# Mask and maximum of attention scores in one VectorE instruction: a two-layer decoder step on one core

## The chip, the core and the metric

The kernel runs on one core of a Trainium2 chip. The metric is the time of the program on the device in microseconds (us). A profile is one execution taken by the hardware profiler; its times count from the start of its span. The engines are named PE (TensorE, matrix products), PEld (TensorE's weight loads), DVE (VectorE), ACT (ScalarE), POOL (GpSimd) and SP (SyncE, which issues most transfers). L2110 is line 2110 of the kernel before.

## The reference

Two decoder layers run over a prompt of 512 tokens and 8 samples of 8 new tokens each. In each layer three mixers read one projection of the normalised input: two gated linear recurrences and a dilated sliding-window attention of 8 heads of 64 channels. A channel mixer follows, dense in layer 0 and with experts in layer 1. The change touches the attention, cut here to what matters; each of three (window, dilation) patterns is one part, and the parts are combined by their softmax denominators:

```
s = einsum(q, k) * HEAD_DIM ** -0.5
s = where(valid, s, -inf)
m = max(s, axis=-1)
p = exp(s - m[..., None])
den = sum(p, axis=-1)
num = einsum(p, v)
```

The samples do the same against a cache of 1024 older keys and values and their own new ones.

## The kernel before

The three dilation patterns are folded into one softmax. The mask holds, for each query and key, the logarithm of the number of patterns in which the key counts, and -1e30 where there is none. These masks are constants in SBUF: `lnc` for the prompt, `smask` for a sample's 1024 cached keys, `smask_new` for the 64 new keys.

Attention is a hand-written schedule. Every engine has its own program, and semaphores tie them together. In each layer all engines run a loop over c = 0 to 9.

- The prompt's work is 16 steps n = 0 to 15: head pair n // 4 and query tile i = n % 4, with 128 (i + 1) keys for each of the two heads. TensorE computes the scores (`prompt_scores`, L1518), VectorE masks and reduces (`prompt_masked`, L2091 and L2093), ACT takes the exponential and its sum (`prompt_exp`, L1056), VectorE divides (`prompt_normed`, L2099 and L2101), TensorE transposes (`prompt_turn`, L1530), ACT copies out of PSUM (`prompt_turned`, L1066), TensorE multiplies with the values (`prompt_values`, L1542). Pass c starts steps 2c and 2c + 1.
- The sample's work is 8 steps b = c: scores against the cached keys (`sample_scores`, L1564), mask and maximum (`sample_masked`, L2108 to L2113), exponential (`sample_exp`, L1078), transposes (`sample_turn`, L1571 and L1574), copies (L1086 and L1087), product with the values (`sample_values`, L1584 and L1589).

Before, a prompt step's scores of both heads are scaled and masked by one `scalar_tensor_tensor` from PSUM into SBUF (tile Pp[i]), which then releases the PSUM scores through the semaphore `sc_free`; TensorE's next `prompt_scores` waits for it. A `tensor_reduce` over both heads follows, waits on `sc_free` too, writes the negated maxima and raises `mx_ready`, for which ACT waits. A sample step does the same over 1024 cached keys, with 64 masked new-key scores copied in behind them, so that its reduction runs over 1088 elements. The new-key scores of all samples are masked once per layer at c = 0 (L2137). TensorE fills gaps there with products whose results nothing reads (`idle_products`, L1290).

The cached keys and values come in pieces of 1 MB, four per sample (two of keys, two of values), through nine buffers; SP issues a piece (L608) when the last reader of its buffer has finished. VectorE also splits finished rows of the mixers into two parts (L2155) after ACT has made the first part (L1126). After the loop the output projection starts.

Of the kernel before, what the change touches and what calls it, by code (L numbers as in the profile page):

```python
# [23 lines left out]
ALU = mybir.AluOpType  # L24
ACT = mybir.ActivationFunctionType
AX = mybir.AxisListType

P = 128
# [121 lines left out]
def log_mult(dist, valid):  # L150
    n = np.where(valid, multiplicity(dist), 0)
    return np.where(n > 0, np.log(np.maximum(n, 1)), -1e30).astype(np.float32)


def shape_constants():
    c = {}
    p = np.arange(P)[:, None]

    u = np.arange(SEQ)[None, :]
    c["lnc"] = log_mult(SEQ - P + p - u, SEQ - P + p - u >= 0)  # L160
    row = p % 32
    t = row % DEC
    live = row < 2 * DEC
    d = PAST + t - np.arange(PAST)[None, :]
    c["smask"] = np.where(live, log_mult(d, d >= 0), 0).astype(np.float32)
    key = np.arange(NS)[None, :]
    new = []
    for b in range(NB):
        d = t - key % DEC
        new.append(np.where(live, log_mult(d, (d >= 0) & (key // DEC == b)), 0).astype(np.float32))  # L170
    c["smask_new"] = np.concatenate(new, 1)
    pos = np.concatenate([np.arange(SEQ), np.tile(PAST + np.arange(DEC), NB)]).astype(np.float32)
    rot_dim = DH // 4
    inv = (np.float32(500000.0) ** (-np.arange(0, rot_dim, 2, dtype=np.float32) / np.float32(rot_dim))).astype(np.float32)
    ang = pos[:, None] * inv[None, :]
    cos, sin = np.ones((P, T), np.float32), np.zeros((P, T), np.float32)
    rot = np.zeros((P, P), np.float32)
    for h in range(2):
        for i in range(rot_dim // 2):
            a, b = h * DH + i, h * DH + rot_dim // 2 + i  # L180
            cos[a] = cos[b] = np.cos(ang[:, i])
            sin[a] = sin[b] = np.sin(ang[:, i])
            rot[b, a] = -1.0
            rot[a, b] = 1.0
    c["cos"], c["sin"], c["rot"] = cos, sin, rot
    q = np.arange(P)[None, :]
    c["mask16"] = ((p // BLK == q // BLK) & (q >= p)).astype(np.float32)
    q = np.arange(NS)[None, :]
    c["mask8"] = ((p // DEC == q // DEC) & (q >= p)).astype(np.float32)
    c["ident"] = np.eye(P, dtype=np.float32)  # L190
    c["ones"] = np.ones((P, P), np.float32)
    c["bones"] = (p // DH == np.arange(P)[None] // DH).astype(np.float32)
    reset = np.ones(T, np.float32)
    reset[0:SEQ:P] = 0
    reset[SEQ::DEC] = 0
    c["reset"] = np.broadcast_to(reset[None], (P, T))
    c["maskb"] = (p // DEC == np.arange(NB)[None]).astype(np.float32)
    c["riota"] = np.broadcast_to(8.0 - np.arange(8)[None], (P, 8))
    c["before"] = (p < np.arange(P)[None]).astype(np.float32)
    c["slots"] = np.broadcast_to(np.arange(MAX_ITEMS)[None], (P, MAX_ITEMS))  # L200
    c["tokens"] = p + P * np.arange(TT + 1)[None]
    for nh in (4, 2):
        c[f"heads{nh}"] = (p // (P // nh) == np.arange(nh)[None]).astype(np.float32)
    q = np.arange(P + BLK - 1)[None, :] - (BLK - 1)
    c["to_row"] = (q == p // 32 * 32).astype(np.float32)
    c["of_row8"] = (p % 32 == np.arange(NS)[None] % DEC).astype(np.float32)
    c["of_row16"] = (p % 32 == np.arange(P)[None] % BLK).astype(np.float32)
    return np.ascontiguousarray(np.concatenate([c[n].astype(np.float32) for n, _ in CONSTS], 1))


def build(nc, d):

    ctx = ExitStack()
    with ctx:
# [3 lines left out]
        def sem(name):  # L218
            return ctx.enter_context(nc.semaphore(name))
# [126 lines left out]

        new_scores = V[:, 0, 0:NB * NS]
        Os = [V[:, 1 + b // 4, b % 4 * P:b % 4 * P + P] for b in range(NB)]
        s_negmax, s_den, s_rden = (SM[:, 2 * k:2 * k + 2] for k in range(3))
        Qs = LIN[:, 6144:7168].rearrange("p (b h q) -> p b h q", b=NB, h=4)  # L350

# [44 lines left out]
        def split(ap):  # L396
# [27 lines left out]
            "upd_done", "s_ready", "vbd_ready", "vbd_used", "supd_done", "sn_ready"))  # L424
        o_done, osq_ready, oss_done, orinv_ready, mixl_ready = (sem(n) for n in (
            "o_done", "osq_ready", "oss_done", "orinv_ready", "mixl_ready"))
        sc_done, sc_free, mx_ready, p_ready, pn_ready, pt_ps, pt_ready, pv_done, mixc_ready = (sem(n) for n in (
            "sc_done", "sc_free", "mx_ready", "p_ready", "pn_ready", "pt_ps", "pt_ready", "pv_done", "mixc_ready"))
        qs_ready, spv_half, os_ready, os_turned = (sem(n) for n in ("qs_ready", "spv_half", "sample_out_ready", "sample_out_turned"))
        ssc_done, ssc_free, smx_ready, sp_ready, spt_ps, spt_ready, spv_done, smix_ready = (sem(n) for n in (  # L430
            "ssc_done", "ssc_free", "smx_ready", "sp_ready", "spt_ps", "spt_ready", "spv_done", "smix_ready"))
        sig_ready = sem("sig_ready")
        mixhi_ready, mixlo_ready, ohi_ready, o_split = (sem(n) for n in (
            "mixed_hi_ready", "mixed_lo_ready", "out_weights_hi_ready", "out_weights_split"))
# [438 lines left out]
        def _(act):  # L873
# [31 lines left out]
            for L in range(DEPTH):  # L905
# [145 lines left out]
                def prompt_exp(n):  # L1051
                    if 0 <= n < N_STEP:
                        i = n % TT
                        act.wait_ge(mx_ready, n0 + n + 1)
                        for h in range(2):
                            op = nc.scalar.activation(Pp[i][:, h, :], Pp[i][:, h, :], ACT.Exp, bias=negmax[:, 2 * i + h:2 * i + h + 1],  # L1056
                                                      accum_out=den[:, 2 * i + h:2 * i + h + 1])
                        op.then_inc(p_ready, 1)

# [15 lines left out]
                def sample_exp(b):  # L1075
                    n = NB * L + b
                    act.wait_ge(smx_ready, n + 1)
                    nc.scalar.activation(Ps, Ps, ACT.Exp, bias=s_negmax[:, b % 2:b % 2 + 1],  # L1078
                                         accum_out=s_den[:, b % 2:b % 2 + 1]).then_inc(sp_ready, 1)

                def sample_turned(b):
# [182 lines left out]
        def _(pe):  # L1264
# [34 lines left out]
            for L in range(DEPTH):  # L1299
# [208 lines left out]
                def prompt_scores(n):  # L1508
                    if 0 <= n < N_STEP:
                        hp, i = n // TT, n % TT  # L1510
                        w = P * (i + 1)
                        if n >= 1:
                            pe.wait_ge(sc_free, n0 + n)
                        for c in range(0, w, 256):
                            e = min(c + 256, w)
                            for h in range(2):
                                r = slice(h * DH, h * DH + DH)
                                op = nc.tensor.matmul(ps[:, h, c:e], QK[r, hp, i * P:i * P + P], QK[r, 4 + hp, c:e],  # L1518
                                                      start=True, stop=True)
                        op.then_inc(sc_done, 1)  # L1520
# [310 lines left out]
        def _(dve):  # L1831
# [47 lines left out]
            for L in range(DEPTH):  # L1879
# [203 lines left out]
                def prompt_masked(n):  # L2083
                    if 0 <= n < N_STEP:
                        i = n % TT
                        w = P * (i + 1)
                        dve.wait_ge(sc_done, n0 + n + 1)
                        if n >= TT:
                            dve.wait_ge(pt_ps, n0 + n - TT + 1)
                        mask = const["lnc"][:, SEQ - w:SEQ].rearrange("p (o s) -> p o s", o=1).to_broadcast([P, 2, w])  # L2090
                        v.scalar_tensor_tensor(Pp[i], ps[:, 0:2, 0:w], DH ** -0.5, mask, ALU.mult, ALU.add).then_inc(sc_free, 1)  # L2091
                        dve.wait_ge(sc_free, n0 + n + 1)
                        v.tensor_reduce(negmax[:, 2 * i:2 * i + 2], Pp[i], AX.X, ALU.max, negate=True).then_inc(mx_ready, 1)  # L2093

                def prompt_normed(n):
                    if 0 <= n < N_STEP:
# [7 lines left out]
                def sample_masked(b):  # L2104
                    n = NB * L + b
                    if b:
                        dve.wait_ge(spt_ps, n)
                    v.tensor_copy(Ps[:, PAST:PAST + NS], new_scores[:, b * NS:b * NS + NS])  # L2108
                    dve.wait_ge(ssc_done, n + 1)
                    v.scalar_tensor_tensor(Ps[:, 0:PAST], ps[:, 4:6, :].rearrange("p a t -> p (a t)"), DH ** -0.5,  # L2110
                                           const["smask"], ALU.mult, ALU.add).then_inc(ssc_free, 1)
                    dve.wait_ge(ssc_free, n + 1)
                    v.tensor_reduce(s_negmax[:, b % 2:b % 2 + 1], Ps, AX.X, ALU.max, negate=True).then_inc(smx_ready, 1)  # L2113

                def sample_out(b):
                    dve.wait_ge(spv_done, NB * L + b + 1)
# [8 lines left out]
                for c in range(NB + 2):  # L2125
                    if c == 0:
# [7 lines left out]
                        prompt_masked(1)  # L2134
                        prompt_normed(0)
                        dve.wait_ge(new_done, L + 1)
                        link(v.scalar_tensor_tensor(new_scores, ps[:, 4, :], DH ** -0.5, const["smask_new"], ALU.mult, ALU.add))  # L2137
                        v.sem_inc(new_ready, 1)
                    if c < NB:
                        sample_masked(c)  # L2140
# [318 lines left out]
```

## Time and profile before

| what | value |
|---|---|
| median of three runs | 2078.82 us (2077.15 to 2086.19) |
| time of the profiled execution | 2080.65 us |
| its span, first to last instruction | 2078.5 us |
| PE busy | 1936.1 us, 93% |
| DVE busy | 1036.6 us, 50% |
| ACT busy | 828.8 us, 40% |
| mean granted TensorE clock | 0.959 of full speed |

Busy shares are means over stages with different limits. The profile also gives the chain of work that ended last, who waited for whom, and the instructions in order of time.

### The profile page before, as it was taken

The numbers are of one execution on the slowest core, as the hardware profiler recorded it, in microseconds if no ns is written. First come the engines' busy times: TensorE is split into PE (matmuls) and PEld (weight loads), VectorE is DVE, ScalarE is ACT, GpSimd is POOL, SyncE is SP. The second block draws the span as 40 slices with busy tenths as digits, with TensorE's granted clock in tenths as the row PEclk, the third lists the DMA queues.
The fourth block names the chain that finished last, engine by engine and source line by source line (L and its number), as shares of the span: only waits on it lengthen the run. The fifth ranks groups of instructions, "written<-read, shape, count | busy, mean of one in ns | idle before, by whom it ended". The sixth has DMA issues, their size and how long they took to land.

```text
span 2078.5 us, 37745 instructions
## 1 busy us (share of the span) xinstructions
PE 1936.1 (93%) x15803; PEld 1706.0 (82%) x15803; DVE 1036.6 (50%) x1355; ACT 828.8 (40%) x1193; POOL 266.5 (13%) x328
## 2 busy tenths in 40 slices
PE   7999788989999999989999789889889999999997
PEld 5999677669999999988899777669767777777775
DVE  5245564663433233324234564673346666667664
ACT  4344322552322122222344322462235666656564
POOL 2000552000100000002000443200300110011100
PEclk9999878999999999999999988999979999999998
DMA  5551201954663466311452200982447877778874
GB/s 186 185 176 64 97 1 41 413 239 158 236 242 102 143 239 242 105 59 51 162 193 106 97 2 3 365 325 86 159 162 252 287 269 277 288 261 285 284 265 119
DMA packets 79950, 375.55 MB, mean 181 GB/s; under 512 B 10160, under 2 KB 10576, under 8 KB 72496
## 3 DMA queue, kind: packets, MB, share of 16 engines
q1 hardware_dynamic: 72528, 354.47, 46.7%
q0 software_dynamic: 7296, 19.23, 3.2%
q8 instruction: 100, 1.64, 0.3%
q14 instruction: 26, 0.21, 0.0%
HBM read 357.21 MB, written 84.37 MB: 212 GB/s over the span
## 4 chain that ended last, share of the span: by engine, by line
PE 80%; DVE 9%; ACT 4%; issue 3%; DMA 2%; POOL 2%; POOLq 0%; SPq 0%; ACTq 0%; DVEq 0%
PE ps L1274 36%; PE ps L1752 17%; PE ps L1759 6%; PE ps L1324 5%; PE ps L1290 4%; PE ps L1268 2%; PE ps L1389 2%; DVE expert_weights_lo L2310 1%; ACT expert_weights_hi L1194 1%; PE ps L1423 1%; DMA normed_or_mixed<-s_hgrn 1%; DVE small L2113 1%; PE ps L1571 1%; DVE scratch L2110 1%; ACT scratch L1056 1%
## 5 line engine op out<-in xcount | busy, mean ns | idle before, releaser
L2310 DVE TENSOR_TENSOR expert_weights_lo<-weight_ring,expert_weights_hi 128x1408 fp32r<-128x1408 f32 (+1 forms) x141 | 203.3, 1475 | 102.2 <-ACT expert_weights_hi L1194 101.7
L1194 ACT ACTIVATE expert_weights_hi<-weight_ring 128x1408 fp32r<-128x1408 f32 (+1 forms) x144 | 178.2, 1262 | 99.5 <-PE ps L1752 99.5
L1274 PE MATMUL ps<-ffn_in_hi,weights_hi 128*128 128x288 f32 x704 | 208.7, 296 | 3.3 <-DVE weights_lo L2185 3.3
L1274 PE MATMUL ps<-ffn_in_lo,weights_hi 128*128 128x288 f32 x704 | 207.7, 295 | 0.0
L1274 PE MATMUL ps<-ffn_in_hi,weights_lo 128*128 128x288 f32 x704 | 207.0, 294 | 0.0
L1274 PE MATMUL ps<-proj_in_hi,proj_weights_hi 128*128 128x288 f32 x608 | 183.8, 302 | 0.0
L1752 PE MATMUL ps<-expert_weights_hi,item_in_hi 128*128 128x352 f32 x512 | 172.8, 338 | 9.1 <-DVE expert_weights_lo L2310 5.4
L1274 PE MATMUL ps<-proj_in_lo,proj_weights_hi 128*128 128x288 f32 x608 | 179.3, 295 | 0.0
L1274 PE MATMUL ps<-proj_in_hi,proj_weights_lo 128*128 128x288 f32 x608 | 178.7, 294 | 0.0
L1752 PE MATMUL ps<-expert_weights_hi,item_in_lo 128*128 128x352 f32 x512 | 167.2, 327 | 0.0
L1752 PE MATMUL ps<-expert_weights_lo,item_in_hi 128*128 128x352 f32 x512 | 166.9, 326 | 0.0
L1290 PE MATMUL ps<-constants 128*128 128x128 f32 x980 | 138.4, 299 | 21.3 <-DMA normed_or_mixed<-s_hgrn 21.3
L1290 PEld LDWEIGHTS ps<-constants 128*128 128x128 f32 x980 | 129.1, 211 | 28.8 <-issue 24.0
L2310 DVE TENSOR_TENSOR expert_weights_lo<-residual,expert_weights_hi 128x1408 fp32r<-128x1408 f32 (+1 forms) x72 | 103.5, 1441 | 80.4 <-ACT expert_weights_hi L1194 80.4
L1274 PEld LDWEIGHTS ps<-ffn_in_hi,weights_hi 128*128 128x128 f32 x704 | 131.9, 187 | 3.8 <-DVE weights_lo L2185 3.8
L2185 DVE TENSOR_TENSOR weights_lo<-weight_ring,weights_hi 128x1024 fp32r<-128x1024 f32 (+1 forms) x60 | 79.5, 1331 | 107.4 <-ACT weights_hi L1144 107.4
L1274 PEld LDWEIGHTS ps<-ffn_in_hi,weights_lo 128*128 128x128 f32 x704 | 132.6, 188 | 0.0
L1274 PEld LDWEIGHTS ps<-ffn_in_lo,weights_hi 128*128 128x128 f32 x704 | 132.2, 188 | 0.0
L1194 ACT ACTIVATE expert_weights_hi<-residual 128x1408 fp32r<-128x1408 f32 (+1 forms) x72 | 88.8, 1234 | 103.5 <-PE ps L1752 103.5
L1752 PEld LDWEIGHTS ps<-expert_weights_hi,item_in_hi 128*128 128x128 f32 x512 | 98.1, 192 | 33.6 <-DVE expert_weights_lo L2310 20.0
L1883 DVE TENSOR_TENSOR proj_weights_lo<-weight_ring,proj_weights_hi 128x1024 fp32r<-128x1024 f32 x54 | 66.8, 1238 | 104.8 <-ACT proj_weights_hi L919 104.6
L1274 PEld LDWEIGHTS ps<-proj_in_hi,proj_weights_hi 128*128 128x128 f32 x608 | 114.0, 187 | 1.8 <-issue 0.8
(351 smaller groups left out, 4399.4 us busy)
## 6 DMA issues: line engine op xcount, KB each, us to landing
weight_ring<-w_gu_moe SPq DMA_DIRECT2D x89, 704.0 KB, 7.0
ok_s<-kcache SPq DMA_DIRECT2D x16, 2032.0 KB, 10.3
ov_s<-vcache SPq DMA_DIRECT2D x16, 2032.0 KB, 10.1
weight_ring<-w_dn_moe SPq DMA_DIRECT2D x55, 512.0 KB, 5.7
residual<-w_gu_moe SPq DMA_DIRECT2D x39, 704.0 KB, 6.5
weight_ring<-w_gu SPq DMA_DIRECT2D x44, 512.0 KB, 4.8
weight_ring<-w_feat SPq DMA_DIRECT2D x38, 512.0 KB, 3.7
residual<-w_dn_moe SPq DMA_DIRECT2D x33, 512.0 KB, 4.3
```

Source lines behind the costliest of these rows:

```text
L1056: op = nc.scalar.activation(Pp[i][:, h, :], Pp[i][:, h, :], ACT.Exp, bias=negmax[:, 2 * i + h:2 * i + h + 1], accum_out=den[:, 2 * i + h:2 ...
L1194: nc.scalar.activation(EWh[:, j % NW, 0:w], slot[:, 0:w], ACT.Copy).then_inc(ew_hi, 1)
L1268: op = nc.tensor.matmul(out_pair[:, a, :], w, rhs[:, a * HALF:a * HALF + HALF], start=k == 0, stop=k == kn - 1)
L1274: op = nc.tensor.matmul(out, x, y, start=k == 0 and n == 0, stop=k == kn - 1 and n == 2)
L1290: nc.tensor.matmul(ps[:, bank, col:col + P], const["ones"], const["ones"], start=True, stop=True, skip_group_check=True)
L1324: op = nc.tensor.matmul(ps[:, n % 8, :], h[x], w[y][:, kk, :], start=k == 0 and m == 0, stop=k == KC - 1 and m == 2)
L1389: return nc.tensor.matmul(ps[0:m, 4 + c, i * w:i * w + w], Kt[:, i - 1, c, 0:m], Qbd[i - 1][:, c * w:c * w + w], start=True, stop=True)
L1752: op = nc.tensor.matmul(out, x[a], w[b][:, o:o + out.shape[-1]], start=first and n == 0, stop=last and n == 2)
L1759: op = nc.tensor.matmul(out[32 * m:32 * m + 32], x, w[:, m * c:m * c + c], start=first, stop=last)
L1883: v.tensor_tensor(Ul[:, u % 2, :], ring[:, (RING0[L] + u) % R, 0:1024], Uh[:, u % 2, :], ALU.subtract).then_inc(u_split, 1)
L2185: v.tensor_tensor(Wl[:, j % NSPLIT, 0:w], ring[:, n % R, 0:w], Wh[:, j % NSPLIT, 0:w], ALU.subtract).then_inc(w_split, 1)
L2310: v.tensor_tensor(EWl[:, j % NW, 0:w], slots[q][:, 0:w], EWh[:, j % NW, 0:w], ALU.subtract).then_inc(ew_split, 1)
```

## The change

Mask, scale and maximum become one instruction, `tensor_tensor_reduce`: it adds the mask to the scores, multiplies by the negated factor -1/8, writes that, and keeps the minimum of the row. The minimum of the negated scores is the negated maximum, as before; the exponential takes the negated scores with scale -1. The mask constants are multiplied by 8 on the host. The instruction keeps one minimum for each partition, so a prompt step takes two of them, one for each head. In a sample step it runs over the 1024 cached keys and starts from the minimum over the new keys, which one added `tensor_reduce` per layer prepares for all samples. `sc_free` and `ssc_free` go; the next prompt scores wait for `mx_ready`.

```
-    c["lnc"] = log_mult(SEQ - P + p - u, SEQ - P + p - u >= 0)
+    c["lnc"] = log_mult(SEQ - P + p - u, SEQ - P + p - u >= 0) * np.float32(DH ** 0.5)
...
-    c["smask"] = np.where(live, log_mult(d, d >= 0), 0).astype(np.float32)
+    c["smask"] = np.where(live, log_mult(d, d >= 0), 0).astype(np.float32) * np.float32(DH ** 0.5)
...
+        new_negmax = SM[:, 8:16]
...
-                            op = nc.scalar.activation(Pp[i][:, h, :], Pp[i][:, h, :], ACT.Exp, bias=negmax[:, 2 * i + h:2 * i + h + 1],
+                            op = nc.scalar.activation(Pp[i][:, h, :], Pp[i][:, h, :], ACT.Exp, bias=negmax[:, 2 * i + h:2 * i + h + 1], scale=-1.0,
...
-                    nc.scalar.activation(Ps, Ps, ACT.Exp, bias=s_negmax[:, b % 2:b % 2 + 1],
+                    nc.scalar.activation(Ps, Ps, ACT.Exp, bias=s_negmax[:, b % 2:b % 2 + 1], scale=-1.0,
...
-                            pe.wait_ge(sc_free, n0 + n)
+                            pe.wait_ge(mx_ready, n0 + n)
...
-                        mask = const["lnc"][:, SEQ - w:SEQ].rearrange("p (o s) -> p o s", o=1).to_broadcast([P, 2, w])
-                        v.scalar_tensor_tensor(Pp[i], ps[:, 0:2, 0:w], DH ** -0.5, mask, ALU.mult, ALU.add).then_inc(sc_free, 1)
-                        dve.wait_ge(sc_free, n0 + n + 1)
-                        v.tensor_reduce(negmax[:, 2 * i:2 * i + 2], Pp[i], AX.X, ALU.max, negate=True).then_inc(mx_ready, 1)
+                        mask = const["lnc"][:, SEQ - w:SEQ]
+                        for h in range(2):
+                            op = v.tensor_tensor_reduce(Pp[i][:, h, :], ps[:, h, 0:w], mask, -DH ** -0.5, 3e38, ALU.add, ALU.min,
+                                                        negmax[:, 2 * i + h:2 * i + h + 1])
+                        op.then_inc(mx_ready, 1)
...
-                    v.scalar_tensor_tensor(Ps[:, 0:PAST], ps[:, 4:6, :].rearrange("p a t -> p (a t)"), DH ** -0.5,
-                                           const["smask"], ALU.mult, ALU.add).then_inc(ssc_free, 1)
-                    dve.wait_ge(ssc_free, n + 1)
-                    v.tensor_reduce(s_negmax[:, b % 2:b % 2 + 1], Ps, AX.X, ALU.max, negate=True).then_inc(smx_ready, 1)
+                    v.tensor_tensor_reduce(Ps[:, 0:PAST], ps[:, 4:6, :].rearrange("p a t -> p (a t)"), const["smask"], -DH ** -0.5,
+                                           new_negmax[:, b:b + 1], ALU.add, ALU.min, s_negmax[:, b % 2:b % 2 + 1]).then_inc(smx_ready, 1)
...
-                        link(v.scalar_tensor_tensor(new_scores, ps[:, 4, :], DH ** -0.5, const["smask_new"], ALU.mult, ALU.add))
+                        link(v.scalar_tensor_tensor(new_scores, ps[:, 4, :], -DH ** -0.5, const["smask_new"], ALU.mult, ALU.subtract))
+                        link(v.tensor_reduce(new_negmax, new_scores.rearrange("p (b s) -> p b s", b=NB), AX.X, ALU.min))
```

## Rows read from the trace of the kernel before

**Rows 1.** The page, chain that ended last, share of the span by engine.
```profile
PE 80%; DVE 9%; ACT 4%; issue 3%; DMA 2%; POOL 2%; POOLq 0%; SPq 0%; ACTq 0%; DVEq 0%
```

**Rows 2.** Busy time by stretches: PE, PEld, DVE, ACT, POOL, clock, DMA share, GB/s.
```profile
384.00:394.00 10.00, 9.33 (x143) 6.38 (x136) 8.44 (x19) 6.65 (x16) 0.00 (x0) 1.00 1.02 420
394.00:404.00 10.00, 9.49 (x143) 6.41 (x139) 7.31 (x12) 6.02 (x17) 0.00 (x0) 1.00 1.01 416
```

**Rows 3.** The chain in order of time, layer 0: start, us, what.
```profile
389.92 1.16 PE ps L1571 x8
...
409.83 0.19 ACT scratch L1078
...
410.07 1.16 PE ps L1571 x8
```

**Rows 4.** VectorE's groups by form: count, busy us, mean ns of one, idle before.
```profile
L2113 DVE TENSOR_REDUCE small<-scratch 128x1 f32<-128x1088 f32 x16 | 20.6, 1286 | 0.5
L2110 DVE SCALAR_TENSOR_TENSOR scratch<-ps,constants 128x1024 f32<-128x1024 f32 x16 | 19.5, 1219 | 10.4 <-PE ps L1564 10.4
...
L2091 DVE SCALAR_TENSOR_TENSOR scratch<-ps,constants 128x1024 f32<-128x1024 f32 x8 | 9.8, 1225 | 7.4 <-DVE small L2148 5.5 <-PE ps L1518 1.9
L2093 DVE TENSOR_REDUCE small<-scratch 128x2 f32<-128x1024 f32 x8 | 9.8, 1220 | 0.3
...
L1920 DVE TENSOR_TENSOR_SCAN linear<-constants,linear 128x576 f32<-128x576 f32 x4 | 5.4, 1357 | 0.1
```

**Rows 5.** One line, L1078 on ACT: durations in ns, min/median/max.
```profile
L1078 ACT ACTIVATION_READ_ACCUMULATOR scratch<-scratch,small x16: 184/186/188, 370.1 to 1388.2; 128x1 f32 x16
```

**Rows 6.** PE's waits, layer 0's attention: us in total, times, longest.
```profile
PE ps L1571 <- ACT scratch L1078: 6.1, 7, 2.6
...
PE ps L1530 <- DVE scratch L2101: 2.0, 2, 1.7
```

**Rows 7.** Instructions in order of time: start us, us, [idle before <-releaser].
```profile
362.91 1.60 PE L1290 MATMUL ps<-constants 128*128 128x128 f32 x12
...
363.05 0.69 DVE L2137 SCALAR_TENSOR_TENSOR values<-ps,constants 128x512 f32<-128x512 f32 x1
...
399.88 0.95 DVE L2091 SCALAR_TENSOR_TENSOR scratch<-ps,constants 128x768 f32<-128x768 f32 x1
...
401.56 1.13 PE L1518 MATMUL ps<-attn_qk 64*128 64x256 f32 x8
...
425.47 0.72 ACT L1056 ACTIVATE scratch<-scratch,small 128x512 f32<-128x512 f32 x1 [0.79 <-DVE small L2093]
...
432.17 1.16 PE L1571 MATMUL ps<-constants,scratch 128*128 128x128 f32 x8 [2.59 <-ACT scratch L1078]
...
447.57 0.72 ACT L1056 ACTIVATE scratch<-scratch,small 128x512 f32<-128x512 f32 x1 [0.78 <-DVE small L2093]
...
451.64 1.97 PE L1530 MATMUL ps<-constants,scratch 128*128 128x128 f32 x8 [1.73 <-DVE scratch L2101]
```

**Rows 8.** Value products in order of time; two issues of value pieces and their landing.
```profile
425.48 1.93 PE L1584 MATMUL ps<-linear,scratch 128*32 128x128 f32 x64
...
437.57 1.93 PE L1584 MATMUL ps<-scratch 128*32 128x128 f32 x64
...
L608 SPq DMA_DIRECT2D linear<-vcache x1: 406/406/406, 406.4 to 406.4; - x1
...
DMA to landing us min/median/max: 17.9/17.9/17.9
...
L608 SPq DMA_DIRECT2D scratch<-vcache x1: 327/327/327, 425.7 to 425.7; - x1
...
DMA to landing us min/median/max: 8.5/8.5/8.5
```

**Rows 9.** Busy time by stretches, end of layer 0's attention, columns as rows 2.
```profile
451.00:452.00 1.00, 0.36 (x2) 0.36 (x3) 0.58 (x2) 0.00 (x0) 0.00 (x0) 0.80 0.00 0
452.00:453.00 1.00, 1.00 (x7) 1.00 (x6) 0.00 (x0) 0.00 (x0) 0.00 (x0) 0.50 0.00 0
```

More of the change, by code:

```diff
@@ L426, in build @@
             "o_done", "osq_ready", "oss_done", "orinv_ready", "mixl_ready"))
-        sc_done, sc_free, mx_ready, p_ready, pn_ready, pt_ps, pt_ready, pv_done, mixc_ready = (sem(n) for n in (
-            "sc_done", "sc_free", "mx_ready", "p_ready", "pn_ready", "pt_ps", "pt_ready", "pv_done", "mixc_ready"))
+        sc_done, mx_ready, p_ready, pn_ready, pt_ps, pt_ready, pv_done, mixc_ready = (sem(n) for n in (
+            "sc_done", "mx_ready", "p_ready", "pn_ready", "pt_ps", "pt_ready", "pv_done", "mixc_ready"))
         qs_ready, spv_half, os_ready, os_turned = (sem(n) for n in ("qs_ready", "spv_half", "sample_out_ready", "sample_out_turned"))
-        ssc_done, ssc_free, smx_ready, sp_ready, spt_ps, spt_ready, spv_done, smix_ready = (sem(n) for n in (
-            "ssc_done", "ssc_free", "smx_ready", "sp_ready", "spt_ps", "spt_ready", "spv_done", "smix_ready"))
+        ssc_done, smx_ready, sp_ready, spt_ps, spt_ready, spv_done, smix_ready = (sem(n) for n in (
+            "ssc_done", "smx_ready", "sp_ready", "spt_ps", "spt_ready", "spv_done", "smix_ready"))
         sig_ready = sem("sig_ready")
```

## The prediction

> **What bounds the kernel now.** I read the page first: of the chain that ended last, TensorE's instructions hold 80% and VectorE's 9% [rows 1], so what a faster mask is worth has to be read in the stage where VectorE's 9% lies. That is attention, once in each of the two layers (357 to 459 us in layer 0, 1303 to 1405 in layer 1). It runs ten passes c; each handles one sample's scores and two prompt steps. In the table by stretches a steady pass shows two things at once: TensorE is busy 9.33 of 10 us, and the core's DMA engines are full (share 1.02, 420 GB/s) with the cached keys and values [rows 2]. VectorE, at 8.44 us and 7.31 in the next, has room.
>
> The chain through a pass reads: the sample's masking L2110, its reduction L2113, the exponential L1078, whose accumulator read ends at 410.02, and then TensorE's transposes L1571 at 410.07; two passes before, these stood at 389.92, so a pass lasts 10.1 us [rows 3]. Both instructions of the sample's mask and maximum lie, then, ahead of a TensorE start. But TensorE had been working on prompt blocks until shortly before. The waits say how much it stood idle: 6.1 us over seven passes at L1571, one of them 2.6 us, and 2.0 us in two waits at L1530 at the end [rows 6]. Layer 1 repeats each of these rows within 0.1 us. These waits are all that the change can take out of TensorE's row.
>
> **The change, part by part.** *Durations.* The sample's pair takes 1.219 + 1.286 us plus 0.02 between them, 2.53 us; the widest prompt pair 1.225 + 1.220, 2.47 us with its gap [rows 4]. L2137 takes 0.69 us for 512 elements [rows 7] and L2110 1.22 for 1024, so the mask instruction costs 1.04 ns an element and 0.15 us fixed.
>
> The trace shows no fused instruction. Its lower bound is the mask instruction alone at 1.04 ns: a TENSOR_REDUCE carries a running maximum over 1088 elements at the same pace [rows 4]. The upper bound is TENSOR_TENSOR_SCAN L1920, which also carries a value along the row: 1.357 us for 576 elements [rows 4], 2.1 ns each after the fixed part. I take the lower end, because a running minimum is what the reduction does, while the scan multiplies and adds. The Trainium skill (DVE: opcode table, instruction layouts, handler registers and perf-mode slots, section 6, Datapath and trigger behaviour) says that a stage reading its own last result has no bubble, and that the built-in scan, which sends it to an earlier stage, runs at half throughput; the scan row agrees.
>
> Writing out the minimum may be a record of its own. Bounds: nothing, or ACT's accumulator read at 0.186 us [rows 5]. I take 0.10, since on ACT the next instruction starts before the read ends. The Trainium skill (VectorE: DVE Perf Modes, section Two Vector instructions with no wait between them) counts an operation with an accumulator output as two instructions; no row here shows that for VectorE.
>
> So the sample's pair goes from 2.53 to 1.32 us: 1.2 saved. A prompt step becomes two instructions of half the width: at 512 each 0.68 + 0.10, less 0.09 of overlap, 1.47 against 2.47: 1.0 saved, at the narrowest width 0.2. Per layer VectorE is relieved of 8 x 1.2 + 4 x (1.0 + 0.7 + 0.45 + 0.2), about 19 us.
>
> *Where it lies on the path.* The sample's 1.2 us is more than the ordinary waits at L1571, on average (6.1 - 2.6) / 6 = 0.6 us, so six of the seven vanish and TensorE runs on without a gap. The long one, 2.59 us at 432.17, hangs on more: VectorE waits there for a mixer split, that for ACT's exponentials from 425.47, and these for the prompt maximum, 0.79 us [rows 7]. The prompt step's 1.0 us takes out those 0.79 and no more, since ACT was busy till then; with the sample's 1.2 that is 2.0 of 2.59. After the last pass L1530 waits 1.73 us at 451.64 behind the same sequence, and ACT's exponential there waited 0.78 [rows 7]: 0.8 more.
>
> *What is late next: the cache pieces.* If the passes shorten, the pieces do not come sooner: the DMA engines are already full, and a piece issued at 406.4 lands 17.9 us later, behind the queue [rows 8]. Buffers that come free earlier only lengthen that queue. This second half of sample 5's values lands at 424.3; L1584 starts at 425.48 [rows 8] and wants its second half 0.9 us later (half of 1.93), at 426.4. Slack: 2.1 us. For sample 6 it is issued at 425.7, lands 8.5 us later at 434.2, and is wanted at 437.57 + 0.9: 4.3 us [rows 8]. The five waits before that are 6.1 less the long one and an ordinary one after it, 3.0 us, and only 2.1 of it can be kept; with 2.0 of the long one, 4.1, under 4.3; with the last ordinary one 4.6; with 0.8 at the end 5.4 per layer.
>
> *The clock.* The granted clock is 0.80 in 451 to 452 and 0.50, the lower level of 1.2 GHz, in 452 to 453 [rows 9]: it fell while TensorE stood idle, and the eight transposes at 451.64 take 1.97 us [rows 7], of which the upper level of 2.4 GHz would give back somewhat under half, 0.9. The idle time before them would shrink from 1.73 to 0.9 us. Yet the 2.59 us at 432.17 brought no fall, so idle time alone doesn't decide; bounds 0 and 0.9 us a layer. I take 0.9: in both layers the fall came when the engine had stood idle for longer than it now would, though nothing in the rows makes this sure.
>
> *Costed at nothing.* The extra reduction over the new keys (512 elements, 0.69 us by L2137's neighbours) stands after L2137, which ends at 363.74; the idle products at 362.91 occupy TensorE until 364.5 [rows 7]. It ends at about 364.45: just covered, and VectorE is 0.2 us earlier by then. Without that cover up to 0.7 us a layer would be lost, since the idle products that follow the first scores are of fixed length. The prompt scores now wait for both minima and not for the mask alone: the mask at 399.88 ended at 400.83, the pair of 384 would end 0.25 us later and starts 1.2 earlier, while the scores it holds start at 401.56 [rows 7]; uncovered it is 0.25 us in each of 15 steps. The scale of -1 on ACT and the constants scaled beforehand add no instruction.
>
> **Sum.** 2 x (5.4 + 0.9) = 12.6 us, less 0.3 for layer 1, whose pieces have a little less slack. The profiled execution took 2080.65 us with a span of 2078.5; its time would be 2068.35. It stands 1.83 above the median of the runs, so the forecast is 2066.5.
>
> **The rivals.**
> *The clock falls as before:* the same, without 1.8 us: 2068.3.
> *No piece is late:* the waits of the first five passes go in full, 0.9 to 1.2 us more a layer: 2064.3. Against it stand the landing rows.
> *The fused instruction costs 0.3 to 0.5 us more than its mask* (read and decoding together). Three of them lie between one pass's scores and the next L1571, two of a prompt step and one of the sample: 0.9 to 1.5 of the 2.2 us saved there are gone. The first five passes keep about 1.6 to 2.3 and the late ones half: 2 to 4 us a layer, 2071 to 2075.
> *It streams at the scan's 2.1 ns:* 1024 elements take 0.15 + 2.15 + 0.1 = 2.4 against 2.53 us, and a prompt pair of 512 2.56 against 2.47. Nothing moves: 2079. For it: it carries a value, as the scan does. Against: the reduction does so too at full pace. The Trainium skill (Vector Engine (DVE) Microarchitecture Reference, section 7, Points that are easy to get wrong) says that the scalar-tensor-tensor layout with two non-bf16 SBUF sources runs at half throughput, for want of a port for the accumulator; here one source is PSUM, and no run yet shows it.
> *Slower: a fixed cost of each fused instruction, on VectorE.* A pass has five of them. VectorE's mean of 7.9 us, less 2.4 saved, plus five times the cost passes today's 10.1 us from 0.9 us on; at 1.2 us a pass takes 11.5, 1.4 more, over 14 passes 20: 2099. Against: the mask instruction's whole fixed part is 0.15 us [rows 4, 7].
>
> **How the numbers follow.** Chances: forecast 0.42, clock falls 0.23, no late piece 0.05, 0.3 to 0.5 us dearer 0.12, half pace 0.12, slower 0.06. A measurement of this kernel tells about 0.5% from no change: 10.4 us, so faster is below 2068.4. Faster gets 0.36 of the first (the rest for a dearer read), half of the second and the third: 0.52. Slower is 0.06, the rest 0.42. The range 2063.5 to 2076 leaves out half pace and slower, nearly 0.2.
>
> **What would show it.** Fused records of 1.2 to 1.4 us for 1024 elements; waits of L1571 for L1078 below 1.5 us a layer in place of 6.1; new waits of L1584 for L608's pieces around sample 5; L1530's last wait at 0.9 us, its block at about 1.1. The forecast is wrong if the fused record is above 1.8 us, if DMA waits pass 2 us a layer, or if the fall of the clock only moves elsewhere.

## The result and the profile after

The changed kernel took 2064.04 us (median of four runs, 2061.35 to 2065.55), the kernel before 2078.16 beside it; the ratio is 0.9922, with a 95% interval of 0.9907 to 0.9938. Against the 2078.82 us at the head of this document that is 2062.6 us. The forecast was 2066.5, its range began at 2063.5: faster, as forecast, but by some 15 to 16 us and not 12.3. The profiled execution took 2063.49 us, with a span of 2061.3 and a mean clock of 0.962.

The chain that ended last, against [rows 1]: VectorE's share fell from 9% to 6%, and DMA's rose from 2% to 5%.

```profile
PE 82%; DVE 6%; DMA 5%; ACT 3%; POOL 2%; issue 2%; SPq 0%; POOLq 0%; ACTq 0%; DVEq 0%
```

Busy time by stretches in the same places as [rows 2]: TensorE is now busy without a gap (10.00 for 9.33 and 9.49), VectorE has 4.78 and 6.77 us in place of 8.44 and 7.31, and the DMA share is as full as it was.

```profile
384.00:394.00 10.00, 10.00 (x153) 6.76 (x149) 4.78 (x20) 7.39 (x19) 0.00 (x0) 1.00 1.02 419
394.00:404.00 10.00, 10.00 (x171) 6.99 (x165) 6.77 (x22) 6.63 (x16) 0.00 (x0) 1.00 1.01 415
```

VectorE's groups by form, against [rows 4]. The fused instruction appears as a custom operation with a read-out record of its own: 1281 ns for 1024 elements, where the pair it replaces took 1219 + 1286.

```profile
L2112 DVE CUSTOM_DVE_ANT_0 scratch<-ps,constants,small 128x1024 f32<-128x1024 f32 x16 | 20.5, 1281 | 11.5 <-PE ps L1565 11.5
...
L2093 DVE CUSTOM_DVE_ANT_0 scratch<-ps,constants 128x512 f32<-128x512 f32 x16 | 10.4, 689 | 17.4 <-issue 14.9 <-PE ps L1519 2.5
...
L2093 DVE CUSTOM_DVE_ANT_0 scratch<-ps,constants 128x128 f32<-128x128 f32 x16 | 4.0, 286 | 2.2 <-PE ps L1519 2.2
...
L2138 DVE TENSOR_REDUCE small<-values 128x8 f32<-128x512 f32 x2 | 1.4, 686 | 0.1
...
L2112 DVE DVE_READ_ACCUMULATOR2_ANT small<- 128x1 f32 x16 | 1.3, 83 | 0.0
```

TensorE's waits in layer 0's attention, against [rows 6]. Lines stand one or two lower than before: L1572 is the sample's transposes (L1571 before), L1531 the prompt's (L1530), L1585 the value products (L1584), L1565 the sample's scores (L1564), L1275 the output projection (L1274). The seven waits of 6.1 us at L1571 are gone. Three waits on value pieces, 1.5 us, are new, and the wait at the head of the output projection went from 1.16 to 1.83 us (in order of time, below).

```profile
PE ps L1275 <- DVE out_weights_lo L2123: 1.8, 1, 1.8
...
PE ps L1531 <- DVE scratch L2103: 1.2, 1, 1.2
PE ps L1585 <- DMA scratch<-vcache: 1.2, 2, 0.8
PE ps L1552 <- DVE linear L2132: 0.4, 1, 0.4
PE ps L1585 <- DMA linear<-vcache: 0.3, 1, 0.3
PE ps L1565 <- DVEq L2139: 0.2, 1, 0.2
```

In order of time: attention's first product, the last step's turns, which before started at 451.64 and took 1.97 us [rows 7], and the start of the output projection.

```profile
357.12 0.80 PE L1519 MATMUL ps<-attn_qk 64*128 64x128 f32 x4 [4.98 <-DVE normed_or_mixed L2079]
...
446.29 1.09 PE L1531 MATMUL ps<-constants,scratch 128*128 128x128 f32 x8 [1.21 <-DVE scratch L2103]
...
452.22 0.40 PE L1275 MATMUL ps<-mixed_hi,out_weights_hi 128*128 128x288 f32 x1 [1.83 <-DVE out_weights_lo L2123]
```

From the first to the last of these attention lasts 95.10 us. The same two starts in the kernel before are 357.00 and 458.45: 101.45 us.

```profile
357.00 0.80 PE L1518 MATMUL ps<-attn_qk 64*128 64x128 f32 x4 [4.97 <-DVE normed_or_mixed L2078]
...
458.45 0.40 PE L1274 MATMUL ps<-mixed_hi,out_weights_hi 128*128 128x288 f32 x1 [1.16 <-DVE out_weights_lo L2123]
```

With layer 1 (101.18 and 95.31) attention gave 12.2 us, 0.1 from the sum's 12.3. But the two spans differ by 17.2 us. The other 5.0 lie where the change touches nothing; the largest piece is in the second layer's linear mixers, where the kernel before ran at the lower clock level in this stretch (PE busy, clock, DMA share):

```profile
1275.00:1280.00 5.00, 5.00 (x25) 0.50 0.00 0
```

Two theories. A: the change acts in attention alone, and the granted clock elsewhere differs from one execution to the next. B: an earlier end of attention also takes time off the untouched stages behind it.

### The profile page after: what moved, and what is told of

It is laid out like the page before. It is cut to its first block, busy times and chain, and to the rows that moved or that the text cites. A ratio compares the mean times of both kernels' runs of the same rounds, so it can differ in the third digit from the quotient of the medians.

```text
span 2061.3 us, 37811 instructions
## 1 busy us (share of the span) xinstructions
PE 1929.4 (94%) x15803; PEld 1699.2 (82%) x15803; DVE 998.4 (48%) x1421; ACT 830.0 (40%) x1193; POOL 267.5 (13%) x328
## 4 chain that ended last, share of the span: by engine, by line
PE 82%; DVE 6%; DMA 5%; ACT 3%; POOL 2%; issue 2%; SPq 0%; POOLq 0%; ACTq 0%; DVEq 0%
PE ps L1275 37%; PE ps L1753 17%; PE ps L1760 6%; PE ps L1325 5%; PE ps L1291 4%; DMA scratch<-vcache 3%; PE ps L1269 2%; PE ps L1390 1%; DVE expert_weights_lo L2311 1%; ACT expert_weights_hi L1195 1%; PE ps L1565 1%; PE ps L1424 1%; DMA normed_or_mixed<-s_hgrn 1%; PE ps L1443 1%; POOL slot_table L824 1%
## 5 line engine op out<-in xcount | busy, mean ns | idle before, releaser
L2311 DVE TENSOR_TENSOR expert_weights_lo<-weight_ring,expert_weights_hi 128x1408 fp32r<-128x1408 f32 (+1 forms) x141 | 203.3, 1475 | 101.2 <-ACT expert_weights_hi L1195 100.7
L1275 PE MATMUL ps<-ffn_in_hi,weights_hi 128*128 128x288 f32 x704 | 208.7, 296 | 4.5 <-DVE weights_lo L2186 3.3
L1275 PE MATMUL ps<-ffn_in_lo,weights_hi 128*128 128x288 f32 x704 | 207.7, 295 | 0.0
L1275 PE MATMUL ps<-ffn_in_hi,weights_lo 128*128 128x288 f32 x704 | 207.0, 294 | 0.0
L1275 PE MATMUL ps<-proj_in_hi,proj_weights_hi 128*128 128x288 f32 x608 | 183.8, 302 | 0.0
L1275 PE MATMUL ps<-proj_in_lo,proj_weights_hi 128*128 128x288 f32 x608 | 179.3, 295 | 0.0
L1275 PE MATMUL ps<-proj_in_hi,proj_weights_lo 128*128 128x288 f32 x608 | 178.7, 294 | 0.0
L1275 PEld LDWEIGHTS ps<-ffn_in_hi,weights_hi 128*128 128x128 f32 x704 | 131.9, 187 | 5.2 <-DVE weights_lo L2186 3.8
L1275 PEld LDWEIGHTS ps<-ffn_in_hi,weights_lo 128*128 128x128 f32 x704 | 132.6, 188 | 0.0
L1275 PEld LDWEIGHTS ps<-ffn_in_lo,weights_hi 128*128 128x128 f32 x704 | 132.1, 188 | 0.0
L1275 PEld LDWEIGHTS ps<-proj_in_hi,proj_weights_hi 128*128 128x128 f32 x608 | 114.0, 187 | 1.8 <-issue 0.8
```

The costliest lines, as they stand in the source:

```text
L1275: op = nc.tensor.matmul(out, x, y, start=k == 0 and n == 0, stop=k == kn - 1 and n == 2)
L2311: v.tensor_tensor(EWl[:, j % NW, 0:w], slots[q][:, 0:w], EWh[:, j % NW, 0:w], ALU.subtract).then_inc(ew_split, 1)
```

## The experiments

Each was measured beside runs of the kernel before. "Attention" is always the time from the first start of L1518's products (or its counterpart) to the first of the output projection, layer 0 and layer 1; "rest" is the span less both.

**The same kernels again.** No edit in `after_again` and `before_again`, `before_look`, `before_look2` and `after_look`. Theory A' in the expectations, here and below, is A with one addition: part of the gain in attention is granted clock that TensorE loses there in the kernel before and not in the changed one. The lengths of attention in the expectations of `before_look`, `after_look` and `idle_fit_before` come from a longer yardstick: what is 101.45 and 101.18 us in the table below is 104.5 and 108.0 there, some 3 us more in layer 0 and 6.8 in layer 1.

> The changed kernel once more, with a second profiled execution. Theory A (chance): attention again ends 6.0 to 6.3 us earlier a layer than in the profile of before, but the second layer's linear mixers need not: their stretch is 0 to 4 us longer than in the first profile of the changed kernel, and the granted clock in it falls somewhere else. Theory B (it follows from the change): the mixers take the same time as in the first profile within 0.5 us, and their clock falls at the same products. The ratio stays within 0.991 to 0.994 by either.

> The kernel before once more, with a second profiled execution. Theory A (chance): the second layer's mixers differ from the first profile of this kernel by more than 1 us somewhere, and the clock does not fall at the same products. Theory B: within 0.5 us in every stage, the same falls at the same products. Ratio 1.000, and its interval shows what five rounds of this kernel can tell.

> A third profile of the kernel before. Theory A': stretches at 0.50 behind the long wait and ahead of the last turns, each there in some executions and layers; attention 104.5 to 107.1 us and 108.0 to 110.8 us. If it never exceeds 104.5 and 108.0 again, the second profile was the odd one.

> A fourth profile of the kernel before, one look. Theory A': attention lasts 101.2 to 101.5 us in a layer where the clock falls only ahead of the last turns, and 104.0 where it also falls behind the long wait and rises late at the entry; no other length.

> A third profile of the changed kernel. Theory A': past the entry no stretch at 0.50 in attention, 98 to 98.3 us and 101.7 to 102.3 us in the two layers.

| profile | attention, layers 0 and 1 | span | rest |
|---|---|---|---|
| before | 101.45, 101.18 | 2078.5 | 1875.9 |
| before_again | 104.01, 103.99 | 2081.1 | 1873.1 |
| before_look | 101.49, 103.98 | 2078.5 | 1873.0 |
| before_look2 | 104.12, 103.93 | 2079.2 | 1871.2 |
| after | 95.10, 95.31 | 2061.3 | 1870.9 |
| after_again | 94.96, 94.95 | 2066.8 | 1876.9 |
| after_look | 95.10, 95.00 | 2062.0 | 1871.9 |

The ratio of `after_again` is 0.9926 (0.9907 to 0.9945), that of `before_again` 0.9998 (0.9987 to 1.001). The rest has a mean of 1873.3 us before and 1873.2 after, so theory B falls, as far as executions whose rest differs by up to 6 us can tell. The stretch of the mixers shown above ran at 1.00 in `before_look`, the same kernel, whose second attention starts at the same time (1303.04 us against 1303.03); it got through 56 products where the first profile had 25:

```profile
1275.00:1280.00 5.00, 5.00 (x56) 1.00 0.00 0
```

Theory A as I had put it falls too, for attention itself has two lengths before: 101.2 to 101.5 us in three layers, 103.9 to 104.1 in five. After, it has one, 95.0 to 95.3. The means, 206.0 and 190.1 us, differ by 15.9, which is what the ratios say (0.9926 of the 2082.4 beside it: 15.4; 0.9922 of 2078.2: 16.2; each interval is some 3 to 4 us to either side). So the expectations of the three further profiles came out: two lengths before, and after no stretch at 0.50 past the entry in `after_look`. In all five long layers the clock is at 0.50 in two places where it is not, or not for so long, in the short ones. Here `before_again`, layer 0, by stretches of two us (PE busy, clock, DMA share): at the entry, where it rose 9 us after the first product and not 5.6; behind the long wait of 2.6 us; and ahead of the last turns, as in [rows 9].

```profile
366.00:368.00 2.00, 2.00 (x12) 0.50 1.00 395
436.00:438.00 2.00, 1.93 (x11) 0.67 1.00 410
457.00:459.00 2.00, 2.00 (x12) 0.54 0.00 0
```

Instructions in order of time, `before_again`: the eight transposes behind the long wait take 1.54 us where [rows 7] has 1.16, and the prompt's turns behind them 1.65 us where the changed kernel's row above has 1.09.

```profile
436.07 1.54 PE L1571 MATMUL ps<-constants,scratch 128*128 128x128 f32 x8 [2.60 <-ACT scratch L1078]
...
438.90 1.65 PE L1530 MATMUL ps<-constants,scratch 128*128 128x128 f32 x8
```

By the start times of ACT's instructions, against layer 0 of `before`, this costs 1.4 us at the entry and 1.4 behind the long wait. At the output projection 2.6 us of it are left: 104.0 us for a long layer against 101.4 for a short one.

**Each half alone.** The edit takes the sample's hunks of the diff, or the prompt's.

> Only the sample's half of the change: the fused instruction at the sample's scores, the prompt's two instructions stay. Theory A (what the change gives is attention's own, 12.1 us in the two profiled executions, and the other 5 us are stages whose granted clock differs from one execution to the next): the waits of the sample's turns on the exponential lose 1.2 us each at most, the ordinary ones (0.6) vanish, the long one loses 1.2, so 4 to 5 us a layer and 0.9 more where the clock no longer falls ahead of the last block: faster by 8 to 11 us, ratio 0.995 to 0.996; most of the gain of both parts. Theory B (whatever makes attention end earlier also takes time off the untouched stages behind it): some 5 us more than A, 13 to 16 us, ratio 0.992 to 0.994.

> Only the prompt's half: the two fused instructions a step at the prompt's scores, the sample's two stay. Theory A: the prompt's 0.79 us a step comes off the waits behind it only where the VectorE queue ahead of the sample's mask is the late one; 2 to 3.5 us a layer with the clock, faster by 4 to 7 us, ratio 0.9966 to 0.998. The two halves then add up to 13 to 18 us or a little more than both together give, because both shorten the same waits and the late cache pieces cap them. Theory B: 5 us more, 9 to 12 us.

`sample_alone`: 0.9935 (0.9916 to 0.9954), 13.5 us; attention 96.24 and 97.19, rest 1869.6. `prompt_alone`: 0.9959 (0.9945 to 0.9974), 8.5 us; attention 98.72 and 98.56, rest 1871.8. The times are nearer to B's figures, but the gain lies within attention (12.6 and 8.8 us under the mean of before), so it is A's place with A's price too low. Against the first profile alone, 202.6 us, it is 9.2 and 5.4, inside A's figures: they had been made from the short execution. The waits in layer 0 show which half does what. The first fence is the sample's half: the wait on the exponential falls from 6.1 to 0.8 us, and the one ahead of the last turns stays at 1.7. The second is the prompt's half: the exponential's wait keeps 3.9 us, and the one ahead of the last turns falls to 1.2.

```profile
PE ps L1531 <- DVE scratch L2102: 2.0, 2, 1.7
...
PE ps L1572 <- ACT scratch L1079: 0.8, 1, 0.8
```

```profile
PE ps L1571 <- ACT scratch L1078: 3.9, 5, 1.7
...
PE ps L1530 <- DVE scratch L2102: 1.2, 1, 1.2
```

Both halves together give less than their sum (15.9 against 21.4). They shorten the same waits: at the exponential the two halves take 5.3 and 2.2 us out of 6.1. In neither half does the clock fall behind the long wait, so both have that gain. The late pieces' share in the difference was not measured apart.

**The length of VectorE's chain.** To the changed kernel, a second issue of each fused instruction, in order:

```
+ link(v.tensor_tensor_reduce(Pp[i][:, h, :], ps[:, h, 0:w], mask, ...))
  op = v.tensor_tensor_reduce(Pp[i][:, h, :], ps[:, h, 0:w], mask, ...)
...
+ link(v.tensor_tensor_reduce(Ps[:, 0:PAST], ps[:, 4:6, :]..., const["smask"], ...))
  v.tensor_tensor_reduce(Ps[:, 0:PAST], ps[:, 4:6, :]..., const["smask"], ...).then_inc(smx_ready, 1)
```

> The changed kernel with each fused instruction issued twice, the second in order behind the first (same result): VectorE's mask and maximum take 3.1 us instead of 1.55 at the prompt's 512 columns and 2.7 instead of 1.36 at a sample, against 2.5 and 2.5 before. Theory A (the length of VectorE's chain from scores to exponential sets the pace of every pass, and the gain was its shortening): the gain turns round, 2 to 6 us a layer slower than the kernel before, ratio 1.002 to 1.006. Rival (VectorE's time is hidden; the gain came of the two waits on a semaphore that the change takes out, or of the scores' bank given back): still faster than before, ratio 0.993 to 0.996.

Ratio 1.0041 (1.0024 to 1.0057), 8.5 us slower than before; attention 108.69 and 107.57, 5.1 a layer over the mean of before. The waits on the exponential are back, and the one on the prompt's minima, which holds up the next scores (L1519), appears:

```profile
PE ps L1572 <- ACT scratch L1079: 7.5, 7, 3.0
...
PE ps L1519 <- DVE small L2095: 2.2, 4, 0.5
```

These two rows make 3.6 us of layer 0's loss. Both layers of this profile are of the long kind, with the clock at 0.50 for 9 us at the entry and again behind the long wait; against the long layers alone the loss is 4.1 us a layer. So the instructions' length is what moves the time; the rival falls.

**The late pieces.** From the tenth piece on, half of each value piece that goes into six of the nine buffers, 22 pieces over both layers (the products then take older numbers in the other half):

```
+ if part >= 2 and at >= NPC and PAIRS <= slot < NPC - 1:
+     dst, src = dst[:, 0:2], src[:, 0:2]
  sp.dma_start(dst, src).then_inc(piece_signal(slot), 16)
```

> The changed kernel; the value pieces from the tenth piece on load only half of their columns blocks (the other half keeps older data, so those products are of other numbers). Theory: the late cache pieces cap the gain as the prediction's step says; without them the waits of the value products on a piece (0.7 to 1.2 us a layer) vanish and the passes ahead of them keep the 0.9 us a layer that the cap took: 1.5 to 3 us faster than the changed kernel, ratio to the kernel before 0.991 to 0.992. Rival (the pieces' waits only take the place of a wait on the exponential that would be there anyway): the same time as the changed kernel within 0.5 us, with the wait on the exponential back.

> The kernel before with the same halved value pieces. Theory: no change (ratio 0.999 to 1.001), since its value products wait for no piece. If it gets faster by more than 1.5 us, transfers held something in the kernel before that its waits do not show, and the comparison of half_values_after says less.

`half_values_before`: 1.0004 (0.9993 to 1.0014), attention 101.41 and 103.94, the same two lengths: as expected. `half_values_after`: 0.9928 (0.9911 to 0.9944), no faster than the changed kernel, so a miss by its time. Its profile shows attention at 93.32 and 93.06, 1.9 us a layer shorter, with no wait on a piece and 0.4 to 0.5 us of wait on the exponential back. In that execution it was lost behind attention: the rest is 1876.5 us, 3.3 over the changed kernel's mean, and the clock was at the lower level for some 3 us in the output projection of both layers, here layer 1's (the changed kernel's first profile has 1.00 there):

```profile
1389.00:1391.00 2.00, 2.00 (x11) 0.50 0.04 8
```

The cap on attention is shown; that lifting it would shorten the kernel is not.

**The clock in the kernel before.** Idle products in TensorE's waits, the two instructions of mask and maximum untouched: 18 ahead of the seventh sample's transposes and 14 ahead of the last turns (`idle_waits_before`), then 10 and 7 (`idle_fit_before`), then these and 21 ahead of attention's first products (`idle_all_before`).

```
+ if b == 6:
+     pe.wait_ge(ssc_free, n + 1)
+     idle_products(18, 4)
  for c in range(8):
...
+ if c == NB:
+     idle_products(14, 5, 256)
  prompt_turn(2 * c - 1)
```

> The kernel before, with 18 idle products in TensorE's long wait on the seventh sample's exponential (2.6 us) and 14 ahead of the last step's turns (1.7 us), both in bank space that nothing reads then; the change itself is not in it. Theory A' (beside the 12 us of shorter waits, part of the gain is that TensorE no longer idles long enough for its clock to fall in attention): the last turns run at the full clock, 1.1 us instead of 1.97, in both layers, and no stretch behind the long wait is at 0.50; the waits themselves stay, so 1.8 us faster than a profile like the first of before, 4 to 5 us faster than one like the second, about 3 us by the medians, ratio 0.998 to 0.999. Rival (the clock falls by the stage's own pattern whatever TensorE does in these two waits): no change, ratio 1.000, falls at 0.50 in the same places.

> The kernel before with idle products that fit into the two waits: 10 (about 2.1 us at the full clock) in the long wait on the seventh sample's exponential, 7 (1.5 us) ahead of the last step's turns. In idle_waits_before the 18 and 14 overran their waits by 1.4 us each, and no stretch at 0.50 was left behind them. Theory A' (part of the gain is granted clock that TensorE loses behind these waits): no stretch at 0.50 there, the attention stage 103 to 104 us in the first layer and 107 in the second, against 104.5 to 107.1 and 108.0 to 110.8 in the profiles of before; 2 to 5 us faster by the medians, ratio 0.9975 to 0.999. Rival (it falls elsewhere in the stage instead): no change, ratio 1.000.

> The kernel before, its two instructions as they were, with idle products in three of TensorE's waits: 21 in the 5 us ahead of attention's first products, 10 in the long wait on the seventh sample's exponential, 7 ahead of the last step's turns. Theory A' (the gain of about 15 us is some 10 us of shorter waits and some 5 us of granted clock, because the kernel before loses the clock behind these waits in attention, and the changed one does not or is covered where it does): attention runs at 1.00 throughout and lasts 99 to 100.5 us a layer in place of 101.2 to 104.0, ratio 0.996 to 0.998; the changed kernel stays 10 us faster than this one. Rival 1 (shorter waits are the whole gain, the second profile of before was a bad one): ratio 0.9985 to 1.000. Rival 2 (the granted clock is most of the gain): ratio 0.994 or below.

| kernel | ratio | attention |
|---|---|---|
| idle_waits_before | 1.0017 (1.0008 to 1.0026) | 103.33, 104.45 |
| idle_fit_before | 0.9984 (0.9972 to 0.9995) | 101.89, 100.32 |
| idle_all_before | 0.9987 (0.9978 to 0.9996) | 99.92, 101.19 |

The first kept the clock at 1.00 behind both waits, but the products outlasted them by 1.4 us each: slower, a miss of mine in sizing. In `idle_fit_before` they fit, and 3.3 us are gained (1.0 to 5.8 by the interval) with every wait of the kernel in place but filled: granted clock alone. No stretch at 0.50 is left behind either wait. Layer 0's 101.89 us are about 1 over the 100 to 101 expected (by the table's measure), since its clock rose only 9 us after the first product (layer 1's after 6); the profile is its slowest execution, with a rest of 1880.7. `idle_all_before` has layer 0 at 1.00 throughout, 99.92 us; in layer 1 the clock still fell, for 3 us from the fifth after the first product, and 101.19 us miss the 99 to 100.5 expected. Its time, 2.7 us faster, lies below what A' gave (4 to 8) and inside rival 1's; its attention, 4.9 us shorter than the mean of before, at A'. In its profile the clock fell instead in the output projection:

```profile
459.00:461.00 2.00, 2.00 (x11) 0.51 0.00 0
```

So by the stage the clock's share is 4 to 5 us, by the time 3. Falls in the output projection, in one layer of each of these two profiles, point the way of the difference; what they cost rests on single executions.

**The entry of the changed kernel.** 21 idle products ahead of attention's first products:

```
+ idle_products(21, 1)
  pe.wait_ge(mixl_ready, 4 * (L + 1))
```

> The changed kernel with 21 idle products (4.5 us) in TensorE's wait ahead of attention (5.0 us), behind which the clock is at 0.50 for 5 to 9 us in every profile. Theory: the stretch at 0.50 goes, the first sample's products come 1 to 1.5 us earlier a layer; of that the late cache pieces, which start with attention and not earlier, let 0 to 1 us a layer through: 0 to 2 us faster than the changed kernel, ratio to before 0.991 to 0.993, and the waits on pieces grow by up to 1 us a layer. Rival (pieces do not bind): 2 to 3 us faster, ratio 0.991, same waits on pieces.

Ratio 0.9917 (0.9900 to 0.9935), not to be told from the changed kernel's, nor by itself from the rival's; attention 95.05 and 95.06, as without, with the clock at 1.00 throughout. The waits on value pieces in layer 0 are 2.2 us in place of 1.5, and the wait on VectorE ahead of the samples' new-key scores (L1552 above) is 1.5 in place of 0.4: these take up what the clock gave. The changed kernel has the reverse by itself, in layer 1 of `after_again`. There the clock rose 9 us after the first product and not 5 to 6, the waits on pieces fell to 0.6 us (in the other five layers they are 1.5 to 1.8), and attention lasted 94.95 us, as ever:

```profile
PE ps L1585 <- DMA linear<-vcache: 0.3, 1, 0.3
PE ps L1585 <- DMA scratch<-vcache: 0.3, 1, 0.3
```

A late rise of the clock at the entry costs the kernel before 1.4 us and the changed one nothing, since its pieces come no earlier.

## Why the prediction was right in its mechanism and short by a term

*Durations: right.* The lower bound was the one to take: 1281 ns for the mask instruction with its running minimum, against 1219 for the mask alone, and 83 ns of read-out where I had 100. Half pace, an instruction 0.3 to 0.5 us dearer than its mask and the fixed cost of 0.9 us fall. The Trainium skill (VectorE: DVE Perf Modes, section Two Vector instructions with no wait between them) counts such an operation as two instructions; the trace agrees, with a record of its own that starts before the first one ends (367.89 against 367.96 us, the first sample's). The half throughput of the Trainium skill (Vector Engine (DVE) Microarchitecture Reference, section 7, Points that are easy to get wrong) does not show here, with one source in PSUM.

*The ordinary waits, the long one and the end: right.* L1571's 6.1 us vanish, where I had left up to 1.5. The last turns wait 1.21 us and not 0.9, their block takes 1.09 as forecast. Unforeseen: 0.16 us at L1565 behind the new reduction, which I had called just covered, and 0.67 us more at the head of the output projection. The latter belongs to the clock: from the start of the last turns the prompt's and samples' last blocks took 5.65 us before and 4.10 after, 1.55 less, of which that wait took back 0.67; it is 1.8 us too in `idle_waits_before`, which has only the clock and not the change.

*The late pieces: right, sized low.* Around sample 5 as worked out, 1.5 us of waits; they cost 1.9 us a layer, where the sum had 0.9 to 1.2.

*The clock: the step that failed.* The 0.9 us at the last turns was right, net of the 0.67: all eight layers of the kernel before show that fall, none of the changed kernel's six. But I read from one execution that the long wait "brought no fall" and set the bounds at 0 and 0.9. In five of eight layers it did bring one, and the clock came back late at the entry besides: 2.6 us each. Over both layers that is 2 x 5/8 x 2.6 = 3.3 us, and 12.3 + 3.3 = 15.6 against the 15.9 of the means. So the sum had 1.8 us of clock, and by the stage it is 5.1; `idle_all_before` gives 4.9. The changed kernel has no long wait to lose the clock behind, and the pieces cover its entry. The sum came within 0.1 us of the first pair of profiles because both start from one execution of the kernel before, with two short layers: the shortest attention of four, in an execution whose rest was longer than the mean by 2.6 us, so its span gave no hint.

*Still open:* why the late rise at the entry and the fall behind the long wait come together, in five layers out of five (and in three more, of `half_values_before` and `fused_twice`), and how much of the clock regained in attention the output projection gives back; the runs show the second in single executions only.

## What to carry to other kernels

Where an engine's wait ends on a chain of two instructions that read the same row, fusing them is worth what the waits behind them hold, not what the engine saves, and the next thing late (here the pieces of a full DMA queue) is to be priced with it. A profile is one draw of the granted clock: before setting bounds, list every wait of the stage after which it could fall, and look at a second profile of the same kernel. A stage whose waits are gone also loses that spread.

## What the runs showed of the hardware beyond the expected

The same program has TensorE's clock fall, or not, behind the same wait of 2.6 us: in five of eight layers, for about 3.4 us at 0.50. Behind the wait of 1.7 us ahead of the last turns it fell in all eight, but behind the same wait in `sample_alone` in one layer of two. Behind a wait of 5.0 us it was always at 0.50 when work began, and stayed there for 5 to 9 us; idle products in the wait kept it at 1.00 (in one layer of four it fell 5 us later). In the second layer's mixers it was at 0.50 from 1275 to 1280 us in one profile and at 1.00 in another, at the same place of the program.
